# Small buffers between the stationary operands: new start addresses in SBUF for a two-layer transformer kernel

## The chip, the cores and the metric

The kernel runs on one core of a Trainium2 chip. The metric is the device time of one execution in microseconds (us), the median of several runs. TensorE is called PE here, its weight loads PEld, VectorE DVE, ScalarE ACT, GpSimd POOL and the queue that issues most transfers SP.

## The reference: what is computed

Two layers, each of a SwiGLU feed-forward block, a mixer with three kinds of attention, and a second feed-forward block, on 256 tokens of width 1024. Cut to what matters:

```python
D_MODEL, SEQ, DEPTH, D_FF = 1024, 256, 2, 2816

def _swiglu(x, w_gate, w_up, w_down):
    return (jax.nn.silu(x @ w_gate) * (x @ w_up)) @ w_down

for l in range(DEPTH):
    x = x + 0.5 * _swiglu(_rmsnorm(x, ffn1_norm[l]), ffn1_w_gate[l], ffn1_w_up[l], ffn1_w_down[l])
    h = _rmsnorm(x, mix_norm[l])
    a_q, a_kv, i_q, i_k, i_w, b_qkv, c_q, c_kv, c_g, m_g = jnp.split(h @ w_in[l], cuts, axis=-1)
    ...   # y_a, y_b, y_c: three attentions, each with its branch matrix
    x = x + (g[:, :, 0] * y_a + g[:, :, 1] * y_b + g[:, :, 2] * y_c) @ w_out[l]
    x = x + 0.5 * _swiglu(_rmsnorm(x, ffn2_norm[l]), ffn2_w_gate[l], ffn2_w_up[l], ffn2_w_down[l])
return _rmsnorm(x, final_norm)
```

All inputs are 32-bit floats.

## The kernel before

**Tiling.** The 256 tokens are two tiles of 128 (`t`). Every weight matrix comes in slabs of 128 partitions x 2048 floats, into one of three slots of `raw`. ACT copies a slab to `whi` (type fp32r) and DVE writes what the copy lost to `wlo`. Each product of the reference is then three matmuls on PE into the same bank of PSUM (`three`, lines 1371 to 1373):

```python
nc.tensor.matmul(o, xh, wh, start=start, stop=False)
nc.tensor.matmul(o, xh, wl, start=False, stop=False)
return nc.tensor.matmul(o, xl, wh, start=False, stop=stop)
```

The first input (`xh`, `xl`) is the stationary operand: 128 columns, 512 bytes in each partition, loaded by a LDWEIGHTS of its own ahead of every matmul. The second (`wh`, `wl`) is the moving operand: mostly 512 columns, 2048 bytes in each partition. A row of the profile such as `ps<-whi,ht_hi` names the moving operand first and the stationary one after it. Beside line 1371 to 1373, line 1421 issues the same product for the first slabs of the program.

**The stationary operands.** There are six: `ht_hi`, `ht_lo` (the normalised, turned activations, 8192 bytes in each partition), `at_hi`, `at_lo` and `bt_hi`, `bt_lo` (the turned activations of a feed-forward step, or turned attention heads, 2048 bytes). `wide` multiplies four pieces of `ht` with a slab. `tall` multiplies two pieces of `at`, `bt` or `ht` with a slab: in `down`, the second to last step of a feed-forward block reads `bt`, the last one `ht`, all others `at`. `branch_c` reads `bt` and `ht`. All slices of the six start at a multiple of 512 bytes from the buffer's start, and so do all slices of 512 columns of `whi` and `wlo`.

**What sets the order.** The program of each engine is written out by hand; semaphores order the engines. Where an SBUF buffer lies follows from the order of the calls of `sb(...)` alone: one after another in each partition, each start rounded up to a multiple of 32 bytes. In the built program `raw` starts at byte 16512, `whi` at 41088 and `wlo` at 65664, all three at 128 modulo 512.

Of the kernel before, what the change touches and what calls it, by code (L numbers as in the profile page):

```python
# [26 lines left out]
F32R = mybir.dt.float32r  # L27
BF16 = mybir.dt.bfloat16
# [5 lines left out]
P = 128  # L34
SEQ, D, DFF, DEPTH = 256, 1024, 2816, 2
NT = SEQ // P
# [7 lines left out]
CPAD = 16  # L44
# [8 lines left out]
NPROJ = M_G  # L53
# [79 lines left out]
def build(nc, x_in, ffn1_w_gate, ffn1_w_up, ffn1_w_down, w_in, cmp_w1_k, cmp_w2_k, cmp_w1_v, cmp_w2_v,  # L133
# [3 lines left out]
    with ctx:  # L137
        def sb(name, shape, dt=F32):
            return ctx.enter_context(nc.sbuf_tensor(name, shape, dt))

        def sem(name):
# [4 lines left out]
        whi = sb("whi", [P, 3, SLAB], F32R)  # L146
        wlo = sb("wlo", [P, 3, SLAB], F32R)
        x = sb("x", [P, NT, D])
        ht_hi = sb("ht_hi", [P, KD, SEQ], F32R)
        ht_lo = sb("ht_lo", [P, KD, SEQ], F32R)  # L150
        at_hi = sb("at_hi", [P, 2, SEQ], F32R)
        at_lo = sb("at_lo", [P, 2, SEQ], F32R)
        scr = sb("scr", [P, 4 * SEQ])
        sg = scr[:, 0:512].rearrange("p (t c) -> p t c", t=NT)
        act = scr[:, 512:1024].rearrange("p (t c) -> p t c", t=NT)

        act_t = scr[:, 0:512].rearrange("p (j c) -> p j c", j=2)
        kvs = scr[:, :].rearrange("p (v g c) -> p v g c", v=2, g=2)
        pr = sb("proj", [P, NT, NPROJ])
        gr = sb("gates", [P, NT * 3 * D])  # L160
        gate = gr[:, :].rearrange("p (t b c) -> p t b c", t=NT, b=3)
        rs = gr[:, 0:NT * NRB * P].rearrange("p (t b c) -> p t b c", t=NT, b=NRB)
# [8 lines left out]


        w1_k = sb("w1_k", [P, 1024])
        w1 = [[v.rearrange("p (j c) -> p j c", j=8) for v in halves] for halves in
              ((w1_k[:, :], gr[:, 512:1536]),
               (prob_all[:, 1024:2048], p_t[:, 0:2, :].rearrange("p f c -> p (f c)")))]
# [1 line left out]
        sc_t = w1_k[:, SEQ:2 * SEQ]  # L178
        qn_t = prob[:, 1, 512:1536].rearrange("p (b c) -> p b c", b=4)

        bt_hi = sb("bt_hi", [P, 2, SEQ], F32R)
        bt_lo = sb("bt_lo", [P, 2, SEQ], F32R)
        cos_s = sb("cos_s", [P, NT, HD])
        sin_s = sb("sin_s", [P, NT, HD])
        rtmp = prob[:, 0, 0:NT * 8 * HD].rearrange("p (t h c) -> p t h c", t=NT, h=8)

        xg = gr[:, D:3 * D].rearrange("p (m c) -> p m c", m=4)
        last_ms = sb("last_ms", [P, 2 * NT])
        warm = sb("warm", [P, 1])
        ident = sb("ident", [P, P])  # L190
        ident_b = sb("ident_b", [P, P], BF16)
        fold = sb("fold", [P, 64])
        cmask = sb("cmask", [P, NT, SEQ])
        kmask_b = sb("kmask_b", [P, NT, CPAD], BF16)
        valid = sb("valid", [P, NT])
        hsel = sb("hsel", [P, 8])
        rows = sb("rows", [112, P])
        cols = sb("cols", [P, 112])
        w2_all = sb("w2_all", [P, DEPTH, 3, HD])
        ssq = sb("ssq", [P, NT])  # L200
        msq = sb("msq", [P, NT])
        mhalf = sb("mhalf", [P, NT])
        rstd = sb("rstd", [P, NT])
        hrstd = sb("hrstd", [P, NT])
        work = sb("work", [P, 384])
        top8 = sb("top8", [P, NT, 8])

        sel_b = sb("sel_b", [P, 384])
        future_b = sb("future_b", [P, 384])
        nmax = sb("nmax", [P, 2, 16])  # L210
        den = sb("den", [P, 2, 16])
        rden = sb("rden", [P, 2, 16])
        cgt = sb("cgt", [P, NT, 24])
        cgt3 = cgt[:, :, :].rearrange("p t (h b) -> p t h b", b=3)
        hid = sb("hid", [P, 64])
        hid2 = sb("hid2", [P, 64])
# [1699 lines left out]
```

## Time and profile before

| | before |
|---|---|
| median of 3 runs | 1164.84 us (1164.72 to 1165.25) |
| span of the profiled execution | 1163.3 us |
| what lies around the span (1164.84 - 1163.3) | 1.5 us |
| PE busy | 1154.6 us, 99% of the span |
| DVE busy | 951.6 us, 82% |
| ACT busy | 582.1 us, 50% |
| DMA | 211.04 MB, mean 181 GB/s |

The profile's page gives the span of one execution, from its first to its last instruction, and its engines' busy time in it. The time of the profiled execution itself isn't listed beside its span, so the span is set against the median. Matmuls overlap in the pipeline, so a matmul's own length (390 ns) is longer than the distance to the next one. What a matmul costs is read from the distance between two starts in the timeline.

### The profile page before, as it was taken

How to read it: one execution, taken by the hardware profiler on the slowest of the kernel's cores; microseconds unless marked ns; L12 is line 12 of the kernel's file. 1: busy time of each engine (PE TensorE's matmuls, PEld its weight loads, DVE VectorE, ACT ScalarE, POOL GpSimd, SP SyncE). 2: the span in 40 equal slices, each digit the busy share in tenths (PEclk: the TensorE clock that was granted, in tenths of full speed). 3: DMA queues.
4: the chain of work that ended last, by engine and by line, in shares of the span. 5: the costliest groups of instructions: out<-in, count | busy, mean ns of one | idle time of the engine just before them, and what ended most of it. 6: DMA issues, size and time to landing. Idle time of an engine off the chain costs nothing.

```text
span 1163.3 us, 16328 instructions
## 1 busy us (share of the span) xinstructions
PE 1154.6 (99%) x5573; PEld 944.9 (81%) x5573; DVE 951.6 (82%) x1788; ACT 582.1 (50%) x757; POOL 31.9 (3%) x67
## 2 busy tenths in 40 slices
PE   9999999999999999999999999999999999999997
PEld 6888888887777888888888888888877788888886
DVE  6877788899977688778887887878999696888777
ACT  6444445447764464344454444454578635434433
POOL 2000000001000000000000000000010000000000
PEclk9999999999999999999999999999999999999999
DMA  8566554765425555655556556456653345655560
GB/s 290 188 210 216 182 191 162 230 203 164 139 76 182 181 159 202 216 193 185 195 176 202 181 171 214 181 189 193 196 178 110 142 137 180 220 180 169 201 235 37
DMA packets 148996, 211.04 MB, mean 181 GB/s; under 512 B 8160, under 2 KB 109136, under 8 KB 148944
## 3 DMA queue, kind: packets, MB, share of 16 engines
q1 hardware_dynamic: 148256, 209.64, 54.5%
q8 instruction: 31, 0.51, 0.2%
q10 hardware_dynamic: 688, 0.71, 0.2%
q14 instruction: 21, 0.17, 0.0%
HBM read 209.28 MB, written 1.05 MB: 181 GB/s over the span
## 4 chain that ended last, share of the span: by engine, by line
PE 99%; DMA 0%; DVE 0%; issue 0%; ACT 0%; POOLq 0%; POOL 0%; ACTq 0%; DVEq 0%
PE ps L1371 30%; PE ps L1373 30%; PE ps L1372 30%; PE ps L1585 2%; PE ps L1641 1%; PE ps L1421 1%; PE ps L1613 1%; PE ps L1390 1%; PE ps L1546 1%; DMA raw<-in_ffn_w_up_dram 0%; PE ps L1558 0%; PE ps L1672 0%; PE ps L1632 0%; DVE x L1000 0%; PE ps L1573 0%
## 5 line engine op out<-in xcount | busy, mean ns | idle before, releaser
L1114 ACT ACTIVATE whi<-raw 128x2048 fp32r<-128x2048 f32 (+1 forms) x195 | 366.0, 1879 | 253.7 <-PE ps L1373 253.2
L536 DVE TENSOR_TENSOR wlo<-raw,whi 128x2048 fp32r<-128x2048 f32 (+1 forms) x195 | 434.0, 2244 | 65.1 <-ACT whi L1114 45.3
L1371 PE MATMUL ps<-whi,ht_hi 128*128 128x512 f32 (+1 forms) x1192 | 465.8, 391 | 0.2
L1373 PE MATMUL ps<-whi,ht_lo 128*128 128x512 f32 (+1 forms) x1192 | 461.0, 387 | 0.0
L1372 PE MATMUL ps<-wlo,ht_hi 128*128 128x512 f32 (+1 forms) x1192 | 460.3, 386 | 0.0
L1373 PEld LDWEIGHTS ps<-whi,ht_lo 128*128 128x128 f32 x1192 | 223.9, 188 | 46.1
L1371 PEld LDWEIGHTS ps<-whi,ht_hi 128*128 128x128 f32 x1192 | 224.0, 188 | 45.2 <-issue 1.4
L1372 PEld LDWEIGHTS ps<-wlo,ht_hi 128*128 128x128 f32 x1192 | 224.1, 188 | 44.0
L598 DVE STREAM_TRANSPOSE scr<-scr 32x128 f32<-32x128 f32 x688 | 208.4, 303 | 10.3
L1371 PE MATMUL ps<-whi,at_hi 128*128 128x512 f32 x304 | 118.5, 390 | 0.0
L1372 PE MATMUL ps<-wlo,at_hi 128*128 128x512 f32 x304 | 118.3, 389 | 0.0
L1373 PE MATMUL ps<-whi,at_lo 128*128 128x512 f32 x304 | 118.3, 389 | 0.0
L1154 ACT ACTIVATE scr<-ps,rstd 128x256 f32<-128x256 f32 x88 | 37.0, 472 | 131.2 <-PE ps L1373 130.7
L588 DVE SCALAR_TENSOR_TENSOR scr<-ps,rstd,scr 128x256 f32<-128x256 f32 x88 | 38.5, 479 | 56.5 <-ACT scr L1154 56.5
L1371 PEld LDWEIGHTS ps<-whi,at_hi 128*128 128x128 f32 x304 | 57.1, 188 | 12.6 <-issue 0.8
L1373 PEld LDWEIGHTS ps<-whi,at_lo 128*128 128x128 f32 x304 | 57.1, 188 | 11.9
L1372 PEld LDWEIGHTS ps<-wlo,at_hi 128*128 128x128 f32 x304 | 57.1, 188 | 11.8
L1247 ACT ACTIVATE prob<-prob,nmax 128x128 f32<-128x128 f32 (+1 forms) x96 | 42.4, 446 | 6.7 <-DVE nmax L751 6.7
L1142 ACT ACTIVATE ht_hi<-ps,cols 128x256 fp32r<-128x256 f32 x47 | 19.2, 472 | 29.9 <-PE ps L1390 29.9
L1213 ACT ACTIVATE proj<-ps,rstd 128x512 f32<-128x512 f32 (+1 forms) x24 | 14.3, 646 | 35.6 <-PE ps L1373 35.6
L1260 ACT ACTIVATE p_t<-ps 128x512 f32<-128x512 f32 x36 | 20.1, 593 | 19.6 <-PE ps L1613 14.2
L560 DVE SCALAR_TENSOR_TENSOR ht_lo<-ps,cols,ht_hi 128x256 fp32r<-128x256 f32 x48 | 20.7, 478 | 10.7 <-ACT ht_hi L1142 10.6
(176 smaller groups left out, 756.0 us busy)
## 6 DMA issues: line engine op xcount, KB each, us to landing
raw<-in_ffn_w_down_dram SPq DMA_DIRECT2D x88, 512.0 KB, 4.9
raw<-in_w_in_dram SPq DMA_DIRECT2D x88, 512.0 KB, 4.4
raw<-in_ffn_w_gate_dram SPq DMA_DIRECT2D x85, 512.0 KB, 4.0
raw<-in_ffn_w_up_dram SPq DMA_DIRECT2D x85, 512.0 KB, 5.0
raw<-in_w_out_dram SPq DMA_DIRECT2D x16, 512.0 KB, 4.4
raw<-in_w_branch_c_dram SPq DMA_DIRECT2D x8, 512.0 KB, 4.4
raw<-in_w_branch_b_dram SPq DMA_DIRECT2D x4, 512.0 KB, 4.0
raw<-in_w_branch_a_dram SPq DMA_DIRECT2D x4, 512.0 KB, 4.0
```

The costliest lines, as they stand in the source:

```text
L536: nc.vector.tensor_tensor(wlo[:, n, 0:w], raw[:, n, 0:w], whi[:, n, 0:w].bitcast(F32), ALU.subtract).then_inc(lo_done, 1)
L560: nc.vector.scalar_tensor_tensor(ht_lo[:, k, :], src, gain(l, n, k), ht_hi[:, k, :].bitcast(F32), ALU.mult, ALU.subtract).then_inc(htl, 1)
L588: nc.vector.scalar_tensor_tensor(act[:, t, :], ps[:, bank, FSTEP:2 * FSTEP], rstd[:, t:t + 1], sg[:, t, :], ALU.mult, ALU.mult).then_inc(a ...
L598: ins = nc.vector.transpose(dst[q:q + 32, :, :, a:a + 32], src[a:a + 32, :, :, q:q + 32])
L1114: nc.scalar.activation(whi[:, n, 0:w], raw[:, n, 0:w], ACT.Copy).then_inc(hi_done, 1)
L1154: nc.scalar.activation(sg[:, t, :], ps[:, t + step_bank(f, i), 0:FSTEP], ACT.Silu, scale=rstd[:, t:t + 1]).then_inc(silu_done, 1)
L1247: ins = nc.scalar.activation(pv, pv, ACT.Exp, scale=-1.0, bias=nmax[:, b, 4 * t + h:4 * t + h + 1], accum_out=den[:, b, 4 * t + h:4 * t + ...
L1260: nc.scalar.activation(p_t[:, f, :], ps[:, pt_bank(e, f), :], ACT.Copy).then_inc(pt_a, 1)
L1371: nc.tensor.matmul(o, xh, wh, start=start, stop=False)
L1372: nc.tensor.matmul(o, xh, wl, start=False, stop=False)
L1373: return nc.tensor.matmul(o, xl, wh, start=False, stop=stop)
L1585: ins = nc.tensor.matmul(score_head(t, h), q_t[row, qb + h // 2, t * P:(t + 1) * P], k_t[row, kb + kstep * (h // 2), 0:nk], start=opens, s ...
```

## The change

Only the order in which SBUF buffers are declared changes. No instruction is added, removed or moved: in both built programs each engine has the same instructions in the same order, and only addresses differ. Small buffers are declared between the six stationary operands, `bt_hi` and `bt_lo` move up beside the other four, and `pr` (named `proj` in the profile), which holds the mixer's projections, moves down behind `w1_k`. The start addresses in the two built programs:

| buffer | before | modulo 512 | modulo 64 | after | modulo 512 | modulo 64 |
|---|---|---|---|---|---|---|
| `whi`, `wlo` | 41088, 65664 | 128 | 0 | the same | 128 | 0 |
| `x` | 90240 | 128 | 0 | the same | 128 | 0 |
| `ht_hi` | 98432 | 128 | 0 | 98816 | 0 | 0 |
| `ht_lo` | 106624 | 128 | 0 | 107072 | 64 | 0 |
| `at_hi` | 114816 | 128 | 0 | 115456 | 256 | 0 |
| `at_lo` | 116864 | 128 | 0 | 117568 | 320 | 0 |
| `bt_hi` | 210784 | 352 | 32 | 119680 | 384 | 0 |
| `bt_lo` | 212832 | 352 | 32 | 121792 | 448 | 0 |
| `scr` | 118912 | 128 | 0 | 123840 | 448 | 0 |
| `proj` | 123008 | 128 | 0 | 193472 | 448 | 0 |
| `gates`, `q_t`, `k_t`, `prob`, `p_t`, `w1_k` | from 145248 | 352 | 32 | from 127936 | 448 | 0 |
| `ident` | 215968 | 416 | 32 | 216768 | 192 | 0 |

The diff:

```diff
@@ -146,17 +146,27 @@
         whi = sb("whi", [P, 3, SLAB], F32R)
         wlo = sb("wlo", [P, 3, SLAB], F32R)
         x = sb("x", [P, NT, D])
+        fold = sb("fold", [P, 64])
+        nmax = sb("nmax", [P, 2, 16])
         ht_hi = sb("ht_hi", [P, KD, SEQ], F32R)
+        top8 = sb("top8", [P, NT, 8])
         ht_lo = sb("ht_lo", [P, KD, SEQ], F32R)
+        cgt = sb("cgt", [P, NT, 24])
         at_hi = sb("at_hi", [P, 2, SEQ], F32R)
+        kmask_b = sb("kmask_b", [P, NT, CPAD], BF16)
         at_lo = sb("at_lo", [P, 2, SEQ], F32R)
+        warm = sb("warm", [P, 1])
+        mhalf = sb("mhalf", [P, NT])
+        bt_hi = sb("bt_hi", [P, 2, SEQ], F32R)
+        ssq = sb("ssq", [P, NT])
+        msq = sb("msq", [P, NT])
+        bt_lo = sb("bt_lo", [P, 2, SEQ], F32R)
         scr = sb("scr", [P, 4 * SEQ])
         sg = scr[:, 0:512].rearrange("p (t c) -> p t c", t=NT)
         act = scr[:, 512:1024].rearrange("p (t c) -> p t c", t=NT)
 
         act_t = scr[:, 0:512].rearrange("p (j c) -> p j c", j=2)
         kvs = scr[:, :].rearrange("p (v g c) -> p v g c", v=2, g=2)
-        pr = sb("proj", [P, NT, NPROJ])
         gr = sb("gates", [P, NT * 3 * D])
         gate = gr[:, :].rearrange("p (t b c) -> p t b c", t=NT, b=3)
         rs = gr[:, 0:NT * NRB * P].rearrange("p (t b c) -> p t b c", t=NT, b=NRB)
@@ -171,6 +181,7 @@
 
 
         w1_k = sb("w1_k", [P, 1024])
+        pr = sb("proj", [P, NT, NPROJ])
         w1 = [[v.rearrange("p (j c) -> p j c", j=8) for v in halves] for halves in
               ((w1_k[:, :], gr[:, 512:1536]),
                (prob_all[:, 1024:2048], p_t[:, 0:2, :].rearrange("p f c -> p (f c)")))]
@@ -178,39 +189,28 @@
         sc_t = w1_k[:, SEQ:2 * SEQ]
         qn_t = prob[:, 1, 512:1536].rearrange("p (b c) -> p b c", b=4)
 
-        bt_hi = sb("bt_hi", [P, 2, SEQ], F32R)
-        bt_lo = sb("bt_lo", [P, 2, SEQ], F32R)
         cos_s = sb("cos_s", [P, NT, HD])
         sin_s = sb("sin_s", [P, NT, HD])
         rtmp = prob[:, 0, 0:NT * 8 * HD].rearrange("p (t h c) -> p t h c", t=NT, h=8)
 
         xg = gr[:, D:3 * D].rearrange("p (m c) -> p m c", m=4)
         last_ms = sb("last_ms", [P, 2 * NT])
-        warm = sb("warm", [P, 1])
         ident = sb("ident", [P, P])
         ident_b = sb("ident_b", [P, P], BF16)
-        fold = sb("fold", [P, 64])
         cmask = sb("cmask", [P, NT, SEQ])
-        kmask_b = sb("kmask_b", [P, NT, CPAD], BF16)
         valid = sb("valid", [P, NT])
         hsel = sb("hsel", [P, 8])
         rows = sb("rows", [112, P])
         cols = sb("cols", [P, 112])
         w2_all = sb("w2_all", [P, DEPTH, 3, HD])
-        ssq = sb("ssq", [P, NT])
-        msq = sb("msq", [P, NT])
-        mhalf = sb("mhalf", [P, NT])
         rstd = sb("rstd", [P, NT])
         hrstd = sb("hrstd", [P, NT])
         work = sb("work", [P, 384])
-        top8 = sb("top8", [P, NT, 8])
 
         sel_b = sb("sel_b", [P, 384])
         future_b = sb("future_b", [P, 384])
-        nmax = sb("nmax", [P, 2, 16])
         den = sb("den", [P, 2, 16])
         rden = sb("rden", [P, 2, 16])
-        cgt = sb("cgt", [P, NT, 24])
         cgt3 = cgt[:, :, :].rearrange("p t (h b) -> p t h b", b=3)
         hid = sb("hid", [P, 64])
         hid2 = sb("hid2", [P, 64])
```

## Rows read from the trace of the kernel before

**Rows 1.** The page of the profiled execution: span, busy shares, PE's granted clock.

```profile
span 1163.3 us, 16328 instructions
...
PE 1154.6 (99%) x5573; PEld 944.9 (81%) x5573; DVE 951.6 (82%) x1788; ACT 582.1 (50%) x757; POOL 31.9 (3%) x67
...
PEclk9999999999999999999999999999999999999999
```

**Rows 2.** The page's chain by engine, and PE's waits by releaser (total, times, longest).

```profile
PE 99%; DMA 0%; DVE 0%; issue 0%; ACT 0%; POOLq 0%; POOL 0%; ACTq 0%; DVEq 0%
...
PE ps L1765 <- DVE scr L975: 1.3, 1, 1.3
PE ps L1772 <- DMA rows<-in_rows_dram: 0.4, 1, 0.4
```

**Rows 3.** Groups of PE by line and form: count, busy us, mean ns, idle before.

```profile
L1371 PE MATMUL ps<-whi,ht_hi 128*128 128x512 f32 x1160 | 457.0, 394 | 0.2
...
L1371 PE MATMUL ps<-whi,at_hi 128*128 128x512 f32 x304 | 118.5, 390 | 0.0
...
L1613 PE MATMUL ps<-ident,prob 128*128 128x128 f32 x144 | 20.2, 276 | 0.0
...
L1371 PE MATMUL ps<-whi,bt_hi 128*128 128x512 f32 x48 | 19.1, 399 | 0.0
...
L1390 PE MATMUL ps<-ident,x 128*128 128x128 f32 x96 | 13.7, 276 | 0.0
...
L1421 PE MATMUL ps<-whi,ht_hi 128*128 128x512 f32 x24 | 7.7, 402 | 0.1
```

**Rows 4.** The same view of PE's weight loads.

```profile
L1371 PEld LDWEIGHTS ps<-whi,ht_hi 128*128 128x128 f32 x1192 | 224.0, 188 | 45.2 <-issue 1.4
...
L1371 PEld LDWEIGHTS ps<-whi,bt_hi 128*128 128x128 f32 x48 | 9.0, 188 | 2.1
```

**Rows 5.** Timeline of PE: start us, length us. Down projections from at, bt, ht.

```profile
565.16 0.39 PE L1371 MATMUL ps<-whi,at_hi 128*128 128x512 f32 x1
...
570.38 0.40 PE L1373 MATMUL ps<-whi,at_lo 128*128 128x512 f32 x1
570.61 0.39 PE L1371 MATMUL ps<-whi,bt_hi 128*128 128x512 f32 x1
570.84 0.40 PE L1372 MATMUL ps<-wlo,bt_hi 128*128 128x512 f32 x1
...
575.98 0.39 PE L1373 MATMUL ps<-whi,bt_lo 128*128 128x512 f32 x1
576.20 0.39 PE L1371 MATMUL ps<-whi,ht_hi 128*128 128x512 f32 x1
```

**Rows 6.** Windows of the same place: busy (count) by engine.

```profile
core 0: us, PE busy (x) PEld busy (x) DVE busy (x) ACT busy (x) POOL busy (x), PEclk, DMA share, GB/s
565.16:570.61 5.45, 5.45 (x25) 4.50 (x24) 5.27 (x15) 2.65 (x3) 0.00 (x0) 1.00 1.06 353
570.61:576.20 5.59, 5.59 (x25) 4.50 (x24) 5.50 (x8) 2.45 (x2) 0.00 (x0) 1.00 0.12 27
```

**Rows 7.** Timeline of PE after a group of transposes in the mixer.

```profile
304.74 0.39 PE L1372 MATMUL ps<-wlo,ht_hi 128*128 128x512 f32 x1
...
305.44 0.39 PE L1372 MATMUL ps<-wlo,ht_hi 128*128 128x512 f32 x1
305.67 0.39 PE L1373 MATMUL ps<-whi,ht_lo 128*128 128x512 f32 x1
...
307.05 0.39 PE L1373 MATMUL ps<-whi,ht_lo 128*128 128x512 f32 x1
307.28 0.81 PE L1632 MATMUL ps<-w_k,scr 128*128 128x256 f32 x3
```

**Rows 8.** Timeline of PE: matmuls of 220 columns.

```profile
244.96 0.27 PE L1373 MATMUL ps<-whi,ht_lo 128*128 128x220 f32 x1
...
249.99 0.28 PE L1373 MATMUL ps<-whi,ht_lo 128*128 128x220 f32 x1
```

## The prediction

> **What bounds the kernel now.** I read the page first: PE is busy 99% of the span, at a granted clock that shows 9 of 10 or more in all 40 slices, its upper level of 2.4 GHz [rows 1]. The chain of work that ended last is PE for 99% too, and the view of waits finds 1.7 us of PE waiting for another engine in the whole execution, both at the start [rows 2]. So DVE, ACT and the transfers set nothing here. The time is the sum of the distances between matmul starts, and only something that alters these distances can alter it.
>
> The groups by form show which distances weigh. Line 1371 has 1160 matmuls of 512 columns from `ht_hi`, 304 from `at_hi` and 48 from `bt_hi`; lines 1372 and 1373 have as many each, and line 1421 has 3 x 24 [rows 3]. That is 3 x (1160 + 304 + 48 + 24) = 4608 matmuls of full width. The groups' mean of some 390 ns is no cost, since neighbours overlap; the timeline gives the cost. From the start at 565.16 to that at 570.38 lie 23 distances, 5.22 us, or 227.0 ns each [rows 5]. 4608 x 227 ns is 1046 us, nine tenths of the span.
>
> One stretch of the same work is slower, and it is the key to this case. From 570.38 to 575.98 lie 24 distances, 5.60 us, or 233.3 ns each [rows 5]. It is the down projection that reads `bt`. Form and code are those of the projection from `at` ahead of it. The first distance of 230 ns or more is the one in which the first `bt` piece is loaded (570.38 to 570.61), and with the load of `ht` for the next projection the short distance comes back (575.98 to 576.20). Other work isn't the reason: the slow stretch has less DMA traffic (27 against 353 GB/s), and about the same share of DVE and ACT, as the fast one in front of it [rows 6]. The load's own length doesn't show it either, 188 ns in both groups [rows 4]. What differs is the address. `bt` starts at 352 modulo 512, and 32 modulo 64; `ht`, `at` and the moving operands `whi` and `wlo` all start at 128 modulo 512, and 0 modulo 64. Where a stationary operand lies does cost time here, some 6.3 ns for each load.
>
> **What the change does, part by part.**
>
> *bt moves to a multiple of 64 bytes.* 3 x 48 = 144 matmuls read it [rows 3]. If the 32 modulo 64 is what costs, they fall from 233.3 to 227.0 ns: 144 x 6.3 ns = 0.91 us less. This stands on PE's chain, so all of it counts.
>
> *ht and at move to other places modulo 512, but stay at 0 modulo 64.* No row of before has a stationary operand at a multiple of 64 that differs from the moving operand's place modulo 512, so the cost is unknown and I bound it. Upper bound: the 6.3 ns of `bt` came from its distance to the moving operand (352 - 128 = 224 bytes), and any distance costs as much. Then 4608 - 144 = 4464 matmuls pay 6.3 ns, +28.1 us, and `bt` keeps its cost. Lower bound: a matmul of 256 columns of plain f32 starts every (0.81 - 0.38) / 2 = 0.215 us while its weights come from `scr` [rows 7] (the merged row holds three of them, and one alone is some 0.38 us long). That is its own streaming time, with nothing on top, so 227 ns contains up to 12 ns which are no streaming if the 512 columns of fp32r need no more than that. If the new places took all of it away, 4608 x 12 ns = 55 us would go. The weight load isn't the limit: matmuls of 220 columns start every (249.99 - 244.96) / 45 = 111.8 ns with the same loads [rows 8]. I take zero, because the row of `at` and `ht` is the nearest: these operands stay multiples of 64, as they are in it, and the change in them is the smaller of the two differences that `bt` shows.
>
> *Matmuls just after transposes.* Behind a group of transposes the distance isn't 227 at once: ten of them take 307.05 - 304.74 = 2.31 us, 231 ns each, not evenly (305.44 to 305.67 is one of the shorter ones), and only then 227 is reached [rows 7]. PE's matmuls of full width fall into 64 unbroken stretches, and I count 5 to 10 such distances in each, so about 64 x 8 x 4 ns = 2.0 us in all. The pattern depends on how weight load and stream fall together, and may shift with the places. I take no change, and plus or minus 2 us for the range.
>
> *Small matmuls and transposes.* `prob` and `ident` lie at 32 modulo 64 before, `x` at 0; transposes of either have the same mean, 276 ns [rows 3]. So moving `prob`, `ident`, `q_t`, `k_t`, `p_t` and `gates` costs nothing that I can see.
>
> *ACT and DVE.* Their largest jobs (making `whi` and `wlo`) keep their addresses. Should the other operands' new places slow an instruction of theirs, PE's 1.7 us of waits say that there is cover now; if it were gone, the next to be late would be the copy of a slab into `wlo`, on which the following matmuls wait.
>
> The sum: 1163.3 us of span - 0.91 = 1162.4, and with the 1.5 us around the span 1163.9 us; against the median of the runs, 1164.84 - 0.91, the same.
>
> **Where the Trainium skill says otherwise.** The row shows 6.3 ns on each load of `bt` [rows 5]. The Trainium skill, "TensorE: Matmul & The Clock Gate", section "Part 2: What happens when you issue a matmul", says that PE has two independent SBUF read ports and that loading the next weights takes no read bandwidth from the running matmul. By that the sum would be 0, and 1164.8 us. It can't be all there is, since the distance changes exactly with the operand that is loaded. "SBUF — State Buffer", section "The DMA port swizzle", gives SBUF lines of 16 bytes. By that `bt` at 32 modulo 64 would be as well aligned as any, the cost would come from its place beside the stream, and the sum would be that of the first rival. No row here shows a line's size.
>
> **The rivals.**
>
> *Slower: distance to the moving operand costs.* The 6.3 ns of `bt` have nothing to do with 64 bytes, but with stream and load starting at different places modulo 512. For it: `bt` differs in that too, and the distances behind transposes (231 ns) show that load and stream disturb each other even where all addresses agree. Against it: nothing but that the alignment explains `bt` as well. Price: 4464 x 6.3 = +28.1 us, 1193.0 us. If only the `lo` operands, a third of the loads, met it, +9.4 us, 1174.2; at the 4 ns of the distances behind transposes, +17.9 us, 1182.7. It decides from 2.3 us / 4464 = 0.5 ns per matmul. Chance 0.28.
>
> *Faster: the common place was itself a collision.* Stream and load both begin at 128 modulo 512, and part of the 12 ns is that. For it: 227 against 215 ns. Against it: `bt` is away from the common place and slower. Price: if each distance fell by 3 ns, half of what `bt` loses, 4608 x 3 ns = -14 us, 1151 us; a third of the loads freed of all 12 ns, 1536 x 12 = -18 us, 1146; all, 1110 us. Chance 0.25.
>
> *Nothing happens,* also to `bt`, since its cost lies in its place in the program: 1164.8 us. Against it speaks the sharp edge at both ends of the stretch. It can't be told from my forecast by the time, only by the rows. Chance 0.07.
>
> **How the numbers follow.** My forecast, alignment to 64 alone, has 0.40. Its own range is 1163.9 plus or minus 2 us for the distances behind transposes, rounded to 1162 to 1166. With the case of nothing it makes 0.47 for within 0.2% (2.3 us, about what a measurement of this kernel can tell from no change). Faster by more has 0.25, slower by more 0.28. The range must reach into both sides: up to 1193, the full price of the first rival, and down to 1146, which leaves out only the deeper half of the faster cases, about 0.1, and a little above 1193.
>
> **What the profile after would show.** Right: the 24 distances of `bt` in each of its stretches sum to 5.45 us instead of 5.60, and those of `at` and `ht` stay at 227.0. First rival: the stretches of `at` and `ht` go to 231 to 235 ns, with the same count of PE instructions and a span longer by the product. Second rival: any distance well below 227 in a long stretch. If `ht_lo` or `at_lo` alone differ, one distance in three changes, the one in which that piece is loaded, which is the distance that starts at line 1372. The forecast is wrong as soon as the distance in the long feed-forward stretches moves by 0.5 ns, since that alone is 2.3 us.

## The result, and the profile after

The changed kernel takes 1190.81 us (median of 5 runs, 1190.21 to 1191.24) against 1164.92 us (5 runs): 25.9 us more, ratio 1.0222, 95% interval 1.0210 to 1.0233. The forecast of 1163.9 us was wrong; the first rival, priced at 1193.0 us, is what happened.

The page after, the lines that answer to [rows 1, 2], and its view of waits:

```profile
span 1188.5 us, 16328 instructions
...
PE 1180.2 (99%) x5573; PEld 947.1 (80%) x5573; DVE 952.0 (80%) x1788; ACT 582.2 (49%) x757; POOL 31.5 (3%) x67
...
PEclk9999999999999999999999999999999999999999
...
PE 99%; DMA 0%; DVE 0%; issue 0%; ACT 0%; POOLq 0%; POOL 0%; DVEq 0%
```
```profile
PE ps L1765 <- DVE scr L975: 1.3, 1, 1.3
PE ps L1772 <- DMA rows<-in_rows_dram: 0.2, 1, 0.2
```

Nothing that a hurried reader looks at has changed: the same 5573 matmuls, the same clock, DVE and ACT with the same busy time (952.0 and 582.2 us), no new wait. PE's busy time alone grew by 25.6 us, from 1154.6 to 1180.2.

The timeline of PE at the down projections that answer to [rows 5]:

```profile
577.24 0.40 PE L1371 MATMUL ps<-whi,at_hi 128*128 128x512 f32 x1
...
582.61 0.39 PE L1373 MATMUL ps<-whi,at_lo 128*128 128x512 f32 x1
582.84 0.40 PE L1371 MATMUL ps<-whi,bt_hi 128*128 128x512 f32 x1
...
588.14 0.39 PE L1373 MATMUL ps<-whi,bt_lo 128*128 128x512 f32 x1
588.37 0.39 PE L1371 MATMUL ps<-whi,ht_hi 128*128 128x512 f32 x1
```

From 577.24 to 582.61 lie 23 distances, 5.37 us, 233.5 ns each, where before `at` had 227.0. From 582.61 to 588.14 lie 24, 5.53 us, 230.4 ns each, where `bt` had 233.3. `ht` is as slow as `at`. In a long stretch of a feed-forward block (the view of windows: length, PE busy and count, PEclk, DMA share, GB/s; PE alone):

```profile
600.00:760.00 160.00, 160.00 (x688) 1.00 0.55 184
```

The same window of the kernel before:

```profile
600.00:760.00 160.00, 160.00 (x707) 1.00 0.57 191
```

688 matmuls in 160 us are 233 ns each, 707 are 226 ns.

**Where the 25.9 us are.** I took every distance between the starts of two consecutive full-width matmuls from both traces: 4543 of them, mean 228.8 ns before and 234.4 ns after, in sum 1039.3 and 1064.9 us. That is +25.6 us. Sorted by the operand that is loaded, `ht` has 20.0 us of it and `at` 6.0, and `bt` gained 0.4. The rest of PE's time, transposes and attention matmuls included, differs by less than 0.5 us. These means include the first distance behind each group of transposes, which is some 316 ns in both kernels.

### The profile page after: what moved, and what is told of

Same layout as the page of the kernel before. It is cut to its first block, busy times and chain, and to the rows that moved or that the text cites. A ratio compares the mean times of both kernels' runs of the same rounds, so it can differ in the third digit from the quotient of the medians.

```text
span 1188.5 us, 16328 instructions
## 1 busy us (share of the span) xinstructions
PE 1180.2 (99%) x5573; PEld 947.1 (80%) x5573; DVE 952.0 (80%) x1788; ACT 582.2 (49%) x757; POOL 31.5 (3%) x67
## 4 chain that ended last, share of the span: by engine, by line
PE 99%; DMA 0%; DVE 0%; issue 0%; ACT 0%; POOLq 0%; POOL 0%; DVEq 0%
PE ps L1371 30%; PE ps L1373 30%; PE ps L1372 30%; PE ps L1585 2%; PE ps L1641 1%; PE ps L1613 1%; PE ps L1421 1%; PE ps L1390 1%; PE ps L1546 1%; PE ps L1558 0%; PE ps L1672 0%; PE ps L1632 0%; DMA rows<-in_rows_dram 0%; DVE x L1000 0%; PE ps L1573 0%
## 5 line engine op out<-in xcount | busy, mean ns | idle before, releaser
L1371 PE MATMUL ps<-whi,ht_hi 128*128 128x512 f32 (+1 forms) x1192 | 474.8, 398 | 0.2
L1373 PE MATMUL ps<-whi,ht_lo 128*128 128x512 f32 (+1 forms) x1192 | 467.1, 392 | 0.0
L1371 PE MATMUL ps<-whi,at_hi 128*128 128x512 f32 x304 | 121.2, 399 | 0.0
```

## The experiments

The shift of a stationary operand beyond the moving one is called r below: its start minus the start of `whi`, in bytes. Before, `ht` and `at` have r = 0 and `bt` r = 224 (modulo 512). In the changed kernel, `ht_hi` and `ht_lo` have 384 and 448, `at` 128 and 192, `bt` 256 and 320. Distances below are means in stretches of full-width matmuls from the 13th distance on, unless a text says otherwise.

Theory 1 is the first rival: what costs is a weight load's place beside the stream. Theory 2 is the forecast's: a stationary operand must start at a multiple of 64.

### Everything moved by 32 bytes

```diff
+        pad_raw = sb("pad_raw", [P, 8])
         raw = sb("raw", [P, 3, SLAB])
```

> The kernel before with 32 bytes of padding ahead of raw: every buffer moves by 32, so the moving and the stationary operands of fp32r all start at 160 modulo 512 and 32 modulo 64, and bt keeps its 224 bytes beyond them modulo 512. Theory 1 (what counts is where a weight load starts beside the moving operand): nothing changes, 227 ns for at and ht, 233 ns for bt, 1164.9 us. Theory 2 (a stationary operand must start at a multiple of 64): at and ht go to 233 ns, 1193 us, and bt, now at 0 modulo 64, falls to 227 ns.

Measured: 1164.79 us against 1165.05, ratio 0.9998 (0.9988 to 1.0007). `at` 226.7 ns, `bt` 233.3 ns, as before. All fp32r operands but `bt` were at 32 modulo 64 and nothing was lost; `bt` was at 0 modulo 64 and nothing was gained. Theory 2 falls here.

### bt declared beside at, nothing between

```diff
         at_lo = sb("at_lo", [P, 2, SEQ], F32R)
+        bt_hi = sb("bt_hi", [P, 2, SEQ], F32R)
+        bt_lo = sb("bt_lo", [P, 2, SEQ], F32R)
         scr = sb("scr", [P, 4 * SEQ])
...
-        bt_hi = sb("bt_hi", [P, 2, SEQ], F32R)
-        bt_lo = sb("bt_lo", [P, 2, SEQ], F32R)
```

> The kernel before with bt_hi and bt_lo declared right behind at_lo and nothing in between: all six stationary operands start at 128 modulo 512, as whi and wlo do. Both theories: bt falls from 233.3 to 227 ns, 144 matmuls, 0.9 us less, 1164.0 us. If the slowness of bt came from its place in the program, nothing changes: 1164.9 us.

Measured: 1163.92 us against 1165.05, ratio 0.9989 (0.9980 to 0.9999); `bt` 226.7 ns. By the distances the 144 loads are worth 144 x 6.6 ns = 0.95 us, which agrees with the prediction's 0.91, and it isn't their place in the program that made them slow.

### Pairs at r = 64, 128, 192, and at 256, 288, 352

```diff
+        pad_ht_hi = sb("pad_ht_hi", [P, 16])
         ht_hi = sb("ht_hi", [P, KD, SEQ], F32R)
         ht_lo = sb("ht_lo", [P, KD, SEQ], F32R)
+        pad_at_hi = sb("pad_at_hi", [P, 16])
         at_hi = sb("at_hi", [P, 2, SEQ], F32R)
         at_lo = sb("at_lo", [P, 2, SEQ], F32R)
+        pad_bt_hi = sb("pad_bt_hi", [P, 16])
+        bt_hi = sb("bt_hi", [P, 2, SEQ], F32R)
+        bt_lo = sb("bt_lo", [P, 2, SEQ], F32R)
```

The second kernel has paddings of 64, 8 and 16 floats in the same three places.

> Hi and lo of each pair start at the same place modulo 512, but ht 64, at 128 and bt 192 bytes beyond the moving operand; all are multiples of 64. Theory 1: at 233 and bt 233 ns, ht between 229 and 233; some 1185 to 1193 us. Theory 2, in the form that the changed kernel leaves it (hi and lo at different places are what costs): all three at 227 ns, 1164 us.

> Pairs together again, ht 256, at 288 and bt 352 bytes beyond the moving operand modulo 512. In the changed kernel ht (384 and 448 beyond) and at (128 and 192 beyond) had the same distances, so theory 1 says that 256 bytes more make no difference: ht 227 ns as with 0; at and bt, at 32 and 96 modulo 256, some 233 ns; 912 matmuls of at and 144 of bt: 1164.9 + 912 x 6.3 ns = 1170.6 us. If the period is 512, ht is not at 227 ns, and the time is up to 1193 us.

Measured, one run each: 1189.71 us with `ht` 233.3 (r = 64), `at` 232.1 (128), `bt` 230.3 ns (192); 1171.05 us with `ht` 226.9 (256), `at` 233.2 (288), `bt` 233.9 ns (352). The loss doesn't need hi and lo apart, since these pairs stand together. `bt` at 192 was lower than I expected. `ht` at 256 is as fast as at 0, which points to a period of 256 bytes.

### Different places modulo 512, the same modulo 256

```diff
         ht_hi = sb("ht_hi", [P, KD, SEQ], F32R)
+        fold = sb("fold", [P, 64])
         ht_lo = sb("ht_lo", [P, KD, SEQ], F32R)
         at_hi = sb("at_hi", [P, 2, SEQ], F32R)
+        hid = sb("hid", [P, 64])
         at_lo = sb("at_lo", [P, 2, SEQ], F32R)
+        hid2 = sb("hid2", [P, 64])
+        bt_hi = sb("bt_hi", [P, 2, SEQ], F32R)
+        bt_lo = sb("bt_lo", [P, 2, SEQ], F32R)
```

(The same three small buffers and `bt` are taken out where they stood.)

> The six stationary operands again at different places modulo 512, but each 0 or 256 bytes beyond the moving operand (ht_hi 0, ht_lo 256, at_hi 256, at_lo 0, bt_hi 256, bt_lo 256), bt beside at, small buffers as filling. Theory 1 with a period of 256 bytes: nothing is lost, 227 ns, 1164 us as with all six at one place. If different places of hi and lo cost by themselves, or the period is 512: 233 ns, up to 1193 us.

Measured: 1163.88 us against 1165.05, ratio 0.9990 (0.9981 to 1.0000); `ht` 226.9, `at` and `bt` 226.7 ns. Small buffers between the stationary operands cost nothing if they fill multiples of 256 bytes.

### The streams moved instead

```diff
+        kmask_b = sb("kmask_b", [P, NT, CPAD], BF16)
         whi = sb("whi", [P, 3, SLAB], F32R)
...
+        cgt = sb("cgt", [P, NT, 24])
         ht_hi = sb("ht_hi", [P, KD, SEQ], F32R)
```

> whi and wlo start 64 bytes later, the six stationary operands keep their place modulo 256 in the partition (128), so that each is 192 bytes beyond the stream modulo 256. Theory 1: as bt in the kernel with pairs at 64, 128 and 192, about 230 ns or more for all: 1164 + 4608 x 3.6 ns = 1181 us. Theory of an operand's own address: 227 ns, 1164 us.

Measured, one run: 1172.38 us; `ht` 229.0, `at` and `bt` 228.9 ns. The stationary operands kept their places modulo 256 and yet got slower, so it is the place beside the stream. The size was off: I had read 230.3 ns for r = 192 from stretches of 24 that had not settled.

### wlo and the lo operands moved together

```diff
+        kmask_b = sb("kmask_b", [P, NT, CPAD], BF16)
         wlo = sb("wlo", [P, 3, SLAB], F32R)
...
+        cgt = sb("cgt", [P, NT, 24])
         ht_hi = sb("ht_hi", [P, KD, SEQ], F32R)
+        top8 = sb("top8", [P, NT, 8])
         ht_lo = sb("ht_lo", [P, KD, SEQ], F32R)
```

(And likewise 192 bytes ahead of `at_hi` and `bt_hi`, 64 ahead of `at_lo` and `bt_lo`.)

> wlo and the three lo operands start 64 bytes further modulo 256, whi and the three hi operands stay together (bt is beside at). A weight load runs while the matmul before it streams: lo loads while wlo streams, hi loads while whi streams. Theory 1a (a load collides with the stream under which it runs): every load has its place beside its stream at 0 modulo 256, so 227 ns everywhere, 1164 us, although hi and lo, and whi and wlo, differ. Theory 1b (what counts is a load's place beside the stream of its own matmul): hi with wlo and lo with whi are 64 apart, two loads of three, so up to 233 ns, 1164 + 2/3 x 29 = 1183 us.

Measured, one run: 1181.76 us, `ht` 231.3, `at` and `bt` 231.1 ns. Theory 1a gave 1164 us and is refuted in this plain form; 1b gave 1183 us. The series of streams and loads that alternate, further down, show that 1b isn't it either.

### Places one by one

Behind the last down projection PE runs series whose results are thrown away, each opened by one transpose (`divide`). The `r` of the code counts floats, so its step of 4 is 16 bytes:

```diff
+            flat = ht_hi[:, :, :].rearrange("p k c -> p (k c)")
+            stream = whi[:, 0, 0:512]
...
+            for r in range(0, 132, 4):
+                divide()
+                for _ in range(36):
+                    nc.tensor.matmul(ps[:, 0, :], flat[:, r:r + P], stream, start=True, stop=True)
```

> All six at one place, and behind the last down projection PE runs 33 series of 36 matmuls of 512 fp32r columns, weights from ht_hi at 0, 16, 32 ... 512 bytes beyond the start of the stream from whi; then weights of 32, 64, 96 columns at 0 and 64 bytes; then plain f32 at 0 and 64; then bf16 at 0 and 64. The results are thrown away. Theory 1: the distance is lowest near 0, 256 and 512 (227 ns), and about 230 to 234 ns between, the same for r and r + 256; fewer weight columns bring it towards 213 ns, since less is loaded beside the stream; plain f32 and bf16 show no difference between 0 and 64, since their streams read half as many bytes in a given time. If the stream alone costs 227 ns, it stays at 227 ns with 32 columns of weights. Rival: with the same stream and weights at each step the places don't matter, all series 227 ns.

The timeline has one row for each series (start, length of all 36). These are r = 0, 64, 144, 256, 320, 400; then 32 columns of weights at r = 0; then bf16 at 0:

```profile
1155.83 8.44 PE L1786 MATMUL ps<-whi,ht_hi 128*128 128x512 f32 x36
...
1189.66 8.65 PE L1786 MATMUL ps<-whi,ht_hi 128*128 128x512 f32 x36
...
1232.19 8.42 PE L1786 MATMUL ps<-whi,ht_hi 128*128 128x512 f32 x36
...
1291.13 8.45 PE L1786 MATMUL ps<-whi,ht_hi 128*128 128x512 f32 x36
...
1324.96 8.64 PE L1786 MATMUL ps<-whi,ht_hi 128*128 128x512 f32 x36
...
1367.47 8.64 PE L1786 MATMUL ps<-whi,ht_hi 128*128 128x512 f32 x36
...
1434.92 8.57 PE L1791 MATMUL ps<-whi,ht_hi 128*32 128x512 f32 x36
...
1547.53 7.93 PE L1800 MATMUL ps<-whi,ht_hi 128*128 128x512 bf16 x36
```

The mean of the last 24 distances of each series, in ns, by r in bytes:

| r | 0 | 16 | 32 | 48 | 64 | 80 | 96 | 112 | 128 | 144 | 160 | 176 | 192 | 208 | 224 | 240 |
|---|---|---|---|---|---|---|---|---|---|---|---|---|---|---|---|---|
| ns | 226.6 | 233.3 | 233.3 | 233.3 | 233.3 | 231.9 | 234.5 | 233.3 | 233.3 | 226.7 | 233.3 | 230.0 | 228.9 | 233.3 | 233.3 | 228.3 |
| ns at r + 256 | 226.7 | 233.3 | 233.3 | 233.3 | 233.3 | 232.0 | 234.4 | 233.3 | 232.6 | 233.3 | 233.3 | 230.0 | 228.9 | 233.3 | 233.3 | 228.3 |

Here is the loss with one stream and one set of weights, and from the second series on with DVE, ACT and POOL idle. 14 of 16 places have the same value 256 bytes on, within 0.2 ns; 128 differs slightly (233.3 and 232.6), and 144 outright (226.7 and 233.3), which I can't explain. A common place gives the lowest value, 226.7, which of the others only r = 144 reaches; most give 233.3. One expectation failed: fewer weight columns don't bring the distance towards 213 ns. At r = 0 they make it longer than with 128 columns (231.7, 230.0 and 230.0 ns with 32, 64 and 96), at r = 64 somewhat shorter (231.7, 232.8 and 228.3 against 233.3). And no place gives 213.3. Plain f32 takes 429.2 ns for each half of a matmul at 0 as at 64, bf16 215.8 ns at both: between these two places they show no difference. Other places weren't tried with them.

### Other lengths, both moved, one element repeated

`series(weights, stream)` is one transpose and then 36 matmuls; `row` is `whi[:, 0, :]`.

```diff
+            for n in (256, 320, 384, 448, 512):
+                for r in (0, 16):
+                    series(flat[:, r:r + P], row[:, 0:n])
+            for move in (4, 8, 16, 32, 36):
+                series(flat[:, move:move + P], row[:, move:move + 512])
+            for r in (0, 16):
+                series(flat[:, r:r + P], row[:, 0:1].broadcast_to([P, 512]))
+            for r in (0, 16):
+                series(flat[:, r:r + 1].broadcast_to([P, P]), row[:, 0:512])
```

> As the kernel with series behind the last down projection, other series of 36 matmuls, results thrown away: streams of 256, 320, 384, 448 and 512 columns, each with the weights at 0 and at 64 bytes beyond the stream; stream and weights both moved by 16, 32, 64, 128 and 144 bytes; a stream that reads one element 512 times, and weights that are one column 128 times, each at 0 and at 64 bytes. Theory 1: at one place 227 ns whatever both are moved by; the 6.7 ns between 0 and 64 bytes is in every length as long as the load runs beside the stream, so from 256 columns on; it vanishes when either side reads one element only, since then no two streams of addresses run against each other. If the 13 ns above 512 / 2.4 GHz = 213.3 ns are the stream's own, they shrink with its length (256 columns: 113 ns); if they are a fixed price of a load, 256 columns take 106.7 + 13.3 = 120 ns. Rival: the collision lies elsewhere (the engine's hand-over from one stream to the next), and one repeated element changes nothing.

Rows of 256 columns at r = 0 and 64, of 512 at 0 and 64, and of the stream of one element at 0 and 64:

```profile
1154.90 4.55 PE L1787 MATMUL ps<-whi,ht_hi 128*128 128x256 f32 x36
...
1159.32 4.36 PE L1787 MATMUL ps<-whi,ht_hi 128*128 128x256 f32 x36
...
1201.98 8.45 PE L1787 MATMUL ps<-whi,ht_hi 128*128 128x512 f32 x36
...
1210.30 8.64 PE L1787 MATMUL ps<-whi,ht_hi 128*128 128x512 f32 x36
...
1260.62 8.12 PE L1787 MATMUL ps<-whi,ht_hi 128*128 128x512 f32 x36
...
1268.60 8.12 PE L1787 MATMUL ps<-whi,ht_hi 128*128 128x512 f32 x36
```

| columns | 256 | 320 | 384 | 448 | 512 |
|---|---|---|---|---|---|
| ns at r = 0 | 120.0 | 146.7 | 173.3 | 202.7 | 226.7 |
| ns at r = 64 | 113.3 | 146.8 | 176.7 | 202.2 | 233.3 |

With 256 columns 64 bytes apart is the better place, so "put them together" is no law: of these lengths it pays at 384 and 512, costs at 256 and changes at most 0.5 ns at 320 and 448. The expectation had asked whether the 13.3 ns above 512 / 2.4 GHz are the stream's own or a fixed price. At r = 0 the excess over columns / 2.4 GHz is 13.3 ns with 256, 320, 384 and 512 columns (16.0 with 448): it doesn't grow with the stream, so a fixed price fits and a share of the stream doesn't.

Moving both by 32, 64 and 128 bytes leaves 226.7 ns; by 16 and 144 it is 231.1, which I had not expected. So the pair's own place counts too; the two slow moves are those that are no multiple of 32, which the start of a whole buffer always is here. A stream that reads one element takes 218.6 and 218.7 ns at the two places: 8 of the 13.3 ns and all of the difference are gone. Weights that are one repeated column take 231.7 and 231.1 ns: the difference between the places is nearly gone here too, but at the slow level. That the stream's reading is what suffers fits these four series, but they don't show it.

### Streams and loads that alternate

```diff
+            for far in (16, 32, 64):
+                series((far, 0), (0, far))
+                series((0, far), (0, far))
+                series((0, far), (0,))
+                series((0,), (0, far))
```

(The first list gives the places of the weights in turn, the second those of the stream, in floats.)

> Series of 48 matmuls behind the last down projection, results thrown away, in which streams or weights alternate between two places, 0 and D, for D = 64, 128 and 256 bytes. First kind: streams alternate, and each load has the place of the stream under which it runs. Second: streams alternate, each load has the place of the stream of its own matmul. Third: the stream stays at 0, the loads alternate. Fourth: the streams alternate, the loads stay at 0. Then fixed streams with the weights 4, 8, 12, 20, 24 and 28 bytes further. Theory 1a (a load collides with the stream under which it runs) says 227 ns for the first kind and some 230 to 233 ns for the second at D = 64 and 128; theory 1b (the stream of its own matmul) the other way round; both say 227 ns for all kinds at D = 256. A third reading, after the kernel with lo and wlo moved together: only an unbroken succession at one place settles at 227 ns, and then both kinds are above it at 64 and 128. For 4 to 28 bytes: if a collision goes by units of 16 bytes, 4 to 12 bytes are between 227 and 233.3 ns (the loads then touch one unit more).

| mean of the last 24, ns | D = 64 | D = 128 | D = 256 |
|---|---|---|---|
| load at the place of the running stream | 233.3 | 230.0 | 226.7 |
| load at the place of its own matmul's stream | 231.7 | 236.7 | 226.7 |
| loads alternate | 232.5 | 233.3 | 226.7 |
| streams alternate | 230.8 | 230.0 | 226.7 |

Neither 1a nor 1b: both kinds are above 226.7 at 64 and 128, and all are at 226.7 at 256. It agrees with the third reading: of these series only those in which streams and loads stay at one place modulo 256 settle at 226.7 ns. Nor can the table of places be averaged for a mixture: in the changed kernel `ht_hi` lies at 128 modulo 256 (233.3 in the table) and `ht_lo` at 192 (228.9), and `ht` takes 233.3 ns. Weights 4, 8, 12, 20, 24 and 28 bytes further gave 232.3, 230.7, 233.3, 233.3, 230.0 and 233.3 ns; no unit can be read from that.

### The changed kernel with its places made equal modulo 256

```diff
+        den = sb("den", [P, 2, 16])
         ht_hi = sb("ht_hi", [P, KD, SEQ], F32R)
         top8 = sb("top8", [P, NT, 8])
+        cgt = sb("cgt", [P, NT, 24])
         ht_lo = sb("ht_lo", [P, KD, SEQ], F32R)
-        cgt = sb("cgt", [P, NT, 24])
         at_hi = sb("at_hi", [P, 2, SEQ], F32R)
         kmask_b = sb("kmask_b", [P, NT, CPAD], BF16)
+        fill_at_lo = sb("fill_at_lo", [P, 48])
         at_lo = sb("at_lo", [P, 2, SEQ], F32R)
...
+        fill_bt_hi = sb("fill_bt_hi", [P, 48])
...
+        fill_bt_lo = sb("fill_bt_lo", [P, 48])
```

> The changed kernel with its whole order of buffers (fold and nmax ahead of ht_hi, proj behind w1_k, and so on) and fuller filling between the stationary operands, so that all six start 0 or 256 bytes beyond the moving operand modulo 512. Theory 1: the whole loss is in the places modulo 256, so 227 ns for ht, at and bt and 1163.9 us, as with bt simply declared beside at. If part of the loss came from the other buffers' moves (proj, gates, prob, ident, or an engine reading them), the time stays above 1165 us by that part.

Measured: 1163.41 us against 1164.92 of the kernel before, ratio 0.9989 (0.9979 to 0.9998), `ht`, `at` and `bt` 226.7 ns. The same window as above shows it (PE alone):

```profile
600.00:760.00 160.00, 160.00 (x707) 1.00 0.57 192
```

The whole loss lay in the places modulo 256, and the rest of the reordering cost nothing that these runs can tell. With all six operands at 0 or 256 bytes `bt` is as fast as the others, and such a kernel is slightly faster than the one before: the three layouts of the kind (1163.92, 1163.88, 1163.41 us) are each about 0.1% below it, with intervals that end at 0.9999, 1.0000 and 0.9998.

## Why the prediction was wrong

**What bounds the kernel** was right: PE alone, by distances; the profile after has no new wait and the same busy time of DVE and ACT.

**bt's row** was read rightly as a cost of an address, 6.3 ns a load. Undone alone it gave 1.1 us with an interval that holds the 0.91 of the first term. The reason given for the term was wrong, though: moving `bt` to a multiple of 64 gives nothing (the kernel moved by 32 bytes has it there, at 233.3 ns). In the changed kernel `bt` lies 0 and 64 bytes beyond the stream modulo 256 and fell to 230.4 ns, 0.4 us in all instead of 0.91.

**The step that failed** is the second term, the change in `ht` and `at`, put at zero: "I take zero, because the row of `at` and `ht` is the nearest: these operands stay multiples of 64, as they are in it, and the change in them is the smaller of the two differences that `bt` shows". `bt` differed in two things, its alignment to 64 and its place beside the stream. I named both and priced both, and then decided by which difference looked smaller, although no row told them apart. The kernel moved by 32 bytes shows that the alignment to 64 is worth nothing, and the pairs, the moved streams and the last kernel show that the place is worth everything: in place of zero, `ht` and `at` cost 26.0 us, from 227 to some 233.4 ns a load.

**The first rival** had mechanism and size: 28.1 us priced, 25.9 measured. It was somewhat too dear because the distances behind transposes were at 231 ns already and had less to lose (the first ten, or all of a shorter one, of each of the 65 stretches, 600 in all, grew by 2.4 ns each, those from the 13th on by 6.1), and because `bt` fell from 233.3 to 230.4 ns instead of staying. Its "any distance costs as much" isn't exact either, as the table of places shows (228 to 234.5 ns).

**The other terms** held. Transposes and small matmuls kept their cost (276 ns for those of `prob`, 111.5 and 111.6 ns between matmuls of 220 columns), ACT and DVE theirs. The distances behind transposes, put at no change within 2 us, grew by 1.5 us; the stretches are 65, not the prediction's 64. The time around the span is 1.75 us where one execution has both numbers (1190.25 and 1188.5), not 1.5, which moves the forecast by a quarter of a microsecond. The faster rival didn't happen: with 512 columns no place was below 226.6 ns. Its premise has something in it, since 8 of the 13.3 ns go when the stream repeats one element, but no place gave them back.

**The rules of the Trainium skill.** The rule that loading weights takes no read bandwidth from the running matmul ("TensorE: Matmul & The Clock Gate", "Part 2") fits bf16 here (215.8 ns at both places tried) and plain f32 (429.2 ns for each half at both). For fp32r the running matmul does lose by the place of the load, 6.7 ns at most places, and the measurement decides. Whether it loses read bandwidth or something else isn't shown.

**What stays open.** Which unit of SBUF or PE the two readings contend for wasn't found. The settled distances of 512 columns are often 34 or 35 times 6.67 ns, which is the time of 16 columns at 2.4 GHz, so stream and load seem to lock to each other; that is argued, not shown. Why r = 144 and 400 differ is open, as is what the 13.3 ns above 213.3 at the common place consist of; they don't grow with the stream's length, and 8 of them go when the stream repeats one element.

## What to carry to other kernels

Where PE is busy 99% with fp32r matmuls of 512 columns and a weight load each, start all stationary and moving operands at the same place modulo 256 bytes, also when small buffers lie between them, and fill to 256 where they don't. For other lengths measure first, since at 256 columns a common place was the slower one. Print the built program's addresses whenever declarations are reordered: no instruction count, wait or clock in the profile shows this loss. PE's busy time shows that there is one, and the distance between matmul starts shows where. When one row differs from its neighbours in two ways, separate the two by a run before forecasting from either, or give them like chances.

## What the hardware showed that I had not expected

- With 512 columns of fp32r the distance depends on the weights' place beside the stream: 226.7 ns at a common place, 228 to 234.5 ns at all others but r = 144, the same 256 bytes on for 14 of 16 places; bf16 (215.8 ns) and plain f32 (429.2 ns for each half) are the same at the two places tried, 0 and 64 bytes.
- The better place depends on the stream's length: with 256 columns, 64 bytes apart is faster (113.3 against 120.0 ns).
- At the common place the excess over columns / 2.4 GHz is 13.3 ns with 256, 320, 384 and 512 columns alike (16.0 with 448).
- Loading fewer weight columns makes it longer at r = 0 (231.7 ns with 32 columns) and a little shorter at r = 64 (228.3 with 96 against 233.3); a stream that reads one element is shorter at both (218.6 ns).
- At one place the distance settles after up to ten matmuls behind a transpose, and then repeats a pattern of 226 and 227 ns.
